# Moving the modulation's weight chunks among the projection loads of a one-core transformer block

## What is computed

```python
mod = silu(c) @ w_ada + b_ada                   # (2048) @ (2048 x 12288): six vectors of 2048
sh_a, sc_a, gt_a, sh_f, sc_f, gt_f = split(mod, 6)
h = rmsnorm(x) * (1 + sc_a) + sh_a
c_q, c_kv, k_pe, q, k, v, z, b, a, gates = split(h @ w_in)
y_a = attention(c_q, c_kv, k_pe) @ w_o_mla      # latent attention, 8 heads
y_b = gated_delta(conv_silu(q, k, v), z, b, a) @ w_o_gdn
x = x + gt_a * ((g_a * y_a + g_b * y_b) @ w_o)
h = rmsnorm(x) * (1 + sc_f) + sh_f
x = x + gt_f * ((silu(h @ gate) * (h @ up)) @ w_down)
```

## Time and profile before

| | us |
|---|---|
| median of 3 runs | 2292.34 |
| the profiled execution's own time | 2293.58 |
| its span, first to last instruction | 2292.3 |
| TensorE busy | 2235.2 (98%) |
| VectorE busy | 1505.7 (66%) |
| ScalarE busy | 1009.0 (44%) |
| DMA queue, share of 16 engines | 65.0% |

### The profile page before, as it was taken

The page is one execution under the profiler, slowest core; times in us unless marked ns, Lnnn a source line. Parts: engine busy times, 40 slices in busy tenths (PEclk is TensorE's granted clock), DMA queues, the critical chain, the costliest instruction groups (busy, mean ns, idle before and its releaser), DMA issues.

```text
span 2292.3 us, 26935 instructions
## 1 busy us (share of the span) xinstructions
PE 2235.2 (98%) x10767; PEld 1855.7 (81%) x10767; DVE 1505.7 (66%) x1927; ACT 1009.0 (44%) x1270; POOL 24.4 (1%) x28
## 2 busy tenths in 40 slices
PE   5998999999999999999999999999999999999998
PEld 3678898888887888888888888887888888888886
DVE  5888898887768777765554555467555555555556
ACT  4345445343444464443344434456444444434444
POOL 0000000000000000000000000000000000000000
PEclk9999999999999999999999999999999999999999
DMA  9966767685678768876555565555555555555553
GB/s 363 381 240 209 245 228 258 198 271 197 220 269 307 275 239 285 273 242 202 184 192 193 184 202 184 191 195 193 191 195 188 188 188 190 187 185 194 197 189 130
DMA packets 276445, 506.75 MB, mean 221 GB/s; under 512 B 24032, under 2 KB 38112, under 8 KB 275296
## 3 DMA queue, kind: packets, MB, share of 16 engines
q1 hardware_dynamic: 276320, 505.03, 65.0%
HBM read 502.51 MB, written 2.49 MB: 220 GB/s over the span
## 4 chain that ended last, share of the span: by engine, by line
PE 82%; DVE 8%; DMA 4%; ACT 2%; issue 2%; SPq 0%; POOL 0%; DVEq 0%; ACTq 0%
PE bank L1200 25%; PE bank L1202 25%; PE bank L1201 25%; DVE WL L1927 3%; PE bank L1391 2%; DMA RAW<-in_w_o_dram 2%; DVE GA L1908 1%; PE bank L1121 1%; ACT WH L1480 1%; PE bank L1212 1%; PE bank L1214 1%; PE bank L1213 1%; DMA RAW<-in_w_o_gdn_dram 1%; PE bank L1148 1%; PE bank L1363 1%
## 5 line engine op out<-in xcount | busy, mean ns | idle before, releaser
L1927 DVE TENSOR_TENSOR WL<-RAW,WH 128x1024 fp32r<-128x1024 f32 (+1 forms) x714 | 864.9, 1218 | 619.2 <-ACT WH L1480 616.5
L1480 ACT CAST WH<-RAW 128x1024 fp32r<-128x1024 f32 (+1 forms) x714 | 743.3, 1047 | 917.6 <-PE bank L1202 733.1
L1200 PE MATMUL bank<-WH,HTh 128*128 128x512 f32 x1936 | 770.4, 398 | 7.3 <-DVE WL L1927 6.5
L1202 PE MATMUL bank<-WH,HTl 128*128 128x512 f32 x1936 | 755.9, 390 | 0.0
L1201 PE MATMUL bank<-WL,HTh 128*128 128x512 f32 x1936 | 755.5, 390 | 0.0
L1200 PEld LDWEIGHTS bank<-WH,HTh 128*128 128x128 f32 x1936 | 364.2, 188 | 88.7 <-DVE WL L1927 11.3
L1201 PEld LDWEIGHTS bank<-WL,HTh 128*128 128x128 f32 x1936 | 364.4, 188 | 77.1 <-issue 4.3
L1202 PEld LDWEIGHTS bank<-WH,HTl 128*128 128x128 f32 x1936 | 364.0, 188 | 76.5
L1908 DVE SCALAR_TENSOR_TENSOR GA<-RAW,ST,GA 128x512 f32<-128x512 f32 x264 | 181.2, 747 | 13.9 <-DMA RAW<-in_w_ada_dram 7.7
L1200 PE MATMUL bank<-WH,R2h 128*128 128x512 f32 x408 | 164.1, 402 | 3.5 <-DVE WL L1927 3.5
L1202 PE MATMUL bank<-WH,R2l 128*128 128x512 f32 x408 | 159.9, 392 | 0.0
(11 more groups left out here) (273 smaller groups left out, 1756.3 us busy)
## 6 DMA issues: line engine op xcount, KB each, us to landing
RAW<-in_a_w_in_dram SPq DMA_DIRECT2D x96, 1024.0 KB, 5.0
RAW<-in_w_gate_up_dram SPq DMA_DIRECT2D x88, 1024.0 KB, 5.0
RAW<-in_w_ada_dram SPq DMA_DIRECT2D x80, 1024.0 KB, 5.2
RAW<-in_w_in_dram SPq DMA_DIRECT2D x63, 1024.0 KB, 5.0
RAW<-in_w_down_dram SPq DMA_DIRECT2D x44, 1024.0 KB, 5.0
RAW<-in_a_w_out_dram SPq DMA_DIRECT2D x32, 1024.0 KB, 5.0
A<-in_w_ada_dram SPq DMA_DIRECT2D x16, 1024.0 KB, 11.7
RAW<-in_w_o_dram SPq DMA_DIRECT2D x16, 1024.0 KB, 5.1
```

Source lines behind the costliest of these rows:

```text
L1200: e.matmul(o, ah[:, s], hi[:, k, :], start=first, stop=False)
L1202: i = e.matmul(o, al[:, s], hi[:, k, :], start=False, stop=last)
L1480: e.copy(hi, rv).then_inc(S["hi"], 1)
L1927: e.tensor_tensor(lo, rv, hi.bitcast(F32), ALU.subtract).then_inc(S["lo"], 1)
```

## The change

Two edits. In `plan_units` the rule "behind every second unit, and behind every unit of the jobs named thick" becomes a table: for each job the number of its quarters, placed behind its last units, or behind every second unit where the number is 2 and the job has four units. In `gate_row` two more slots pass before the gate's product.

```diff
-        thick = (("conv", 3), ("conv", 4), ("og", 2), ("og", 3))
+        quarters = {"conv": (0, 0, 0, 1, 1, 3), "ga": (3, 3, 2, 3), "z": (3, 3), "gb": (3, 3, 3, 3), "og": (1, 1, 2, 2), "wo": (2, 2, 0, 0),
+                    "uqn": (0, 0), "uqp": (0,), "ukk": (0, 0), "ukv": (0, 0)}
         for k, (j, t0) in enumerate(order):
             u.append(("w", j, t0, min(j.step, j.nkt - t0)))
-            never = (("ga", 2), ("gb", 3)) if extra and extra[0][1] < 20 else (("wo", 3), ("gate", 0))
-            if extra and (k % 2 or (j.name, j.c) in thick) and (j.name, j.c) not in never:
+            if j.name in quarters:
+                units = j.nkt // j.step
+                wanted = t0 // j.step >= units - quarters[j.name][j.c] if quarters[j.name][j.c] != 2 or units == 2 else k % 2
+            else:
+                wanted = k % 2 and (j.name, j.c) != ("gate", 0)
+            if extra and wanted:
                 u.append(extra.pop(0))
@@ def gate_row(self, ci):
-        for n in range(4):
+        for n in range(6):
             if n == 2:
                 self.put("ga_sum", ci)
             yield
```

## The result

The changed kernel takes **2301.36 us** (median of 6 runs, 2299.1 to 2302.64), the kernel before 2292.52 us beside it: ratio 1.0034, 95% interval 1.0023 to 1.0044. That is slower, by about 8 us, where 2283 was forecast. Its profiled execution took 2300.79 us, 7.2 us more than the one of before. In the rows of after every line number of before is 5 higher (1200 is 1205, 1927 is 1932).

The account below looks back on a forecast made before the run. TensorE, busy 98%, was taken as the bound, with only hidden waits to win, VectorE being short up to `conv` 5. Terms -16.3 + 3.5 + 0.5 + 0.5 + 1.5 + 0.7 = -9.6 us gave 2283 us, range 2279 to 2287.

Parts of the forecast that it names:

- Part 1: Quarters leave the stretch up to `conv` 5, so its waits shrink: -16.3 us, bounds 13 and 19.
- the 159 us of work: TensorE's estimated work without waits in the first stretch of 180.2 us, leaving 21 us as waits.
- Part 2: Quarters enter the stretch from `conv` 5 to `gb`; VectorE fits on average, with local costs: +4.5 us.
- The larger of "2.73 - 0.4" and "5.5 - 2.0": TensorE's wait at `ga` 2 and `om` 2, from quarters ahead of splits with little spare time: +3.5 us, lower bound 0.
- `conv` 5 and `ga` 0: One more quarter each where VectorE was nearly full, but splits begin far ahead: +0.5 us, between 0 and 2.
- The cells: A quarter between cell steps can delay VectorE's result that TensorE needs: +0.5 us, between 0 and 4.
- The places beside `ga` 2: One quarter ahead of the split of `ga` 2's fifth half, one ahead of `om` 2's first; 0.4 us to spare.
- Parts 3 and 4: In `og` and `wo`, earlier quarters on busy DMA engines, and the gate's product behind `mix` transposes: +2.2 us.
- The bank's wait: At `og`, the gate's first product waits for the bank the `mix` transposes took: +0.7 us, bounds 0 and 3.2.
- The slower case: In `ga` 1, stores block refilling of three RAW buffers: 22 us cost against 16.3, 2298 us; chance 0.05.
- The case that all is covered: Later stretches hide the added quarters: gain 16.3, cost 1, time 2277 us; chance 0.17.
- over 8 us of waits between `conv` 5 and `og`: Sign that the forecast is wrong: TensorE's waits for WL, or of cell steps, total over 8 us there.

Follow-up runs that it names:

- half the arithmetic: Changed kernel with half of each of VectorE's multiply-adds left out for chunks from 8 on, loads kept: 2297.58 us, ratio 1.0012.
- half the bytes: Changed kernel with half of each quarter's load left out (0.5 MB in place of 1 MB), multiply-adds kept: 2299.57 us, ratio 1.0022.
- the last kernels: Changed kernel with five RAW buffers and cell stores on GpSimd: 2280.0 us; also with `ga` 2's quarters in the `z` jobs and the gate's product bank changed: 2278.84 us.
- five buffers, middle: Changed kernel with two more RAW buffers, only from `conv` 5's fifth half to `gb` 0's ninth: 2293.36 us, ratio 0.9995.
- the kernel with another bank: Changed kernel with the gate's product in a bank that no transpose group just took: 2300.46 us, ratio 1.0028.
- the kernel with the last chunk later: Changed kernel with one quarter fewer beside `og` 2 and one more beside `wo` 2, three RAW buffers: 2299.9 us, ratio 1.0024.

## Why the prediction was wrong

**Part 1 was right in size, and not quite in kind.** -16.1 us against -16.3. But 2.5 of it are three products of `mod` that now run later. The working put them into the 159 us of work, and then never took them to the next stretch: a term of +2.5 us was missing in the sum. The waits gained are 13.6 us, near the lower bound of 13. That the total came out within 0.2 us is luck.

**Part 2 is the step that failed**: +4.5 forecast, 16.5 us of waits measured (19.0 with the products), because it took loads to be in time that three buffers could not keep in time. The larger of "2.73 - 0.4" and "5.5 - 2.0" was read from the spare time of splits in the earlier trace rows. That counts a quarter as 2.73 us in VectorE's order, and takes every load to be there when its turn comes. Where loads are in time (five buffers, stores on GpSimd), the same quarters in the same order cost `ga` 2 1.2 us, 0.8 of it the product; so +3.5 was even too much for what it priced.

What it left out was the ring. From rows: a load lands after 5.2 us, and a unit then has a cast of 1.05 and two splits of 1.22 behind it, 8.7 us for its place; a quarter has 5.3 and 2.73, 8.0 us. By that estimate a `ga` job before (four units, two quarters) took 50.8 us of places, with three buffers 16.9 of its 21.8 us. With three quarters it takes 58.8, or 19.6, and only when every split comes at once. The reserve fell from 4.9 to 2.2 us a job, and the stores stop the queue for 7.5 us. The same estimate with five buffers is 11.8 of 21.8 us. `gb` 3 bears it out: with three quarters it takes 21.8 us as before, but it is entered with 1.9 us of lead and left with 0.2, and with five buffers with 5.4 and 4.5. What the estimate does not give is why half the arithmetic helps more than half the bytes.

- `conv` 5 and `ga` 0, +3.3 for +0.5: "they now begin with splits far ahead" did not come: at the first half of `conv` 5 the lead is 3.6 us, before it was 3.8, and at the fifth half it is 0.1. Five buffers take 1.7 of it; 1.5 are left, in which stands the 0.9 us of waiting for a split that the last kernels still show. The rest was not tried apart.
- The cells, +0.5: `om` 0 lost 3.1 us and `ga` 1 none. With five buffers `om` 0 takes 16.2 as before, so that was the ring too. `z` 0 is the place where the mechanism named here was right, with 1.4 us.
- The places beside `ga` 2 were misread: in the kernel's order its two quarters stand ahead of the splits of its third and seventh halves, not ahead of its fifth and of `om` 2's first, and the half with 0.4 us to spare is the eighth. Both quarters then lie ahead of that half, and the working would have given 5.5 - 0.4 = 5.1 us in place of 3.5. It is not what made the sum 12 us too small.
- The price of `ga` 2 is a sum of two: the empty lead at its start and the queue behind the stores. The one alone gives back 3.7 (five buffers, middle), the other 5.0, both 7.7 of 8.9.

**Parts 3 and 4**, +2.2 forecast, +4.4 measured. The bank's wait (+0.7) was 6.2 us, above its bound of 3.2, which rested on two splits ahead of the remainder in the earlier trace rows with their loads landed. Yet it was 1.5 us of cost of its own at most, by the kernel with another bank. What `og` and `wo` lose is the lead with which they are entered. The place of the quarters as such costs 0.9 us there: 141.0 against 140.2 with five buffers.

**The rivals.** The slower case had the right mechanism (three RAW buffers, a queue that stands still behind the stores), the wrong job (`ga` 1, which cost nothing) and a chance of 0.05. It was set aside because the stores cost nothing in the trace of before. That row showed what they cost at a lead of over 5 us, and the change took that lead away. Its own condition, "if the lead at 405 us is under some 5 us", did not come true at the first stores and did at the second. The lead was the thing to work out, and the earlier trace rows had the start of it: 38.1 us of waiting for loads against 84.9 us for places. The case that all is covered is what five buffers and free stores come near to. Among the signs named ahead, "over 8 us of waits between `conv` 5 and `og`" and "a granted clock under 1.00" from `ga` to `gb` both came.

That DMA bandwidth itself is the limit at `og` has not held. In the kernel with five buffers and the stores on GpSimd the queue is as full as in the earlier trace rows, from 664 to 700 us,

```profile
q1 hardware_dynamic: 5507, 13.22, 98.2%
```

367 GB/s, and TensorE waits 1.1 us there. The loads were asked for earlier, not more quickly served.

## What to carry to other kernels

Before work is moved into a stretch that looks to have room, count what each piece holds, not only what it keeps busy: a load buffer is taken from the issue to the last read, and (landing + use) x loads / buffers against the time of the stretch says roughly whether the lead can be won back (it ranked half the bytes and half the arithmetic wrongly here). A wait that costs nothing in a trace may cost nothing only because of a lead; read what the lead is, and whether the change eats it. And a large named wait that goes away without the time going away marks where lateness surfaced: ask what was late upstream before mending it.

## What was not expected of the hardware

- Small stores cost their issuer: 16 stores of 4 KB hold SyncE's queue for 7.54 us, 0.47 us each, as long as the landing of a 1 MB load and half again. With more buffers this alone was 4.4 us (27.3 to 22.9 in `ga` 2); issued by GpSimd, the same stores took 4.03 us for eight and held up no load. The Trainium skill, DMA: Bandwidth & Descriptors, section "Issuing engines are not separate DMA queues", says that a second issuer saves only the sequencer's time, "which is usually small relative to the DMA itself". The trace agrees with the first half; here the time of issue was the larger one (a store of 4 KB lands after 2.4 us, sixteen take 7.5 to issue), and it was other loads that paid.
- A load of 512 KB lands after 3.7 us, one of 1 MB after 5.3: half the bytes save 1.6 us.
- A wait of 2.3 us of TensorE cost 4.1 us and one of 6.2 us some 8.0 (an estimate: `og` 1 took 8.5 us more than in the kernel with the last chunk later, 0.5 of them the product). Behind them the granted clock was 0.68 for 5.4 us and 0.51 for 3.5 us though TensorE was busy, which is 1.7 us each time.
